# Squares of the query and key tiles: from GpSimd to ScalarE, straight from PSUM

## The reference

```
qkv = rmsnorm(x, norm_mix[0]) @ w_qkv                     # 512 x 3072
q, k -> 8 heads x 2 maps x 64 channels
q = partial_rope(rmsnorm(q, q_gain), cos, sin)            # rms over 64 channels
k = partial_rope(rmsnorm(k, k_gain), cos, sin)
a = softmax(q0 k0 / 8) - lam * softmax(q1 k1 / 8);  o = a @ v
```

## Time and profile before

| | |
|---|---|
| median of 3 runs | 981.86 us |
| lowest and highest | 980.97 and 982.65 us |
| the profiled execution | 980.41 us |
| its span, first to last instruction | 978.7 us |
| TensorE busy | 966.7 us (99%) |
| VectorE busy | 850.8 us (87%) |
| ScalarE busy | 464.0 us (47%) |
| GpSimd busy | 379.5 us (39%) |

### The profile page before, as it was taken

How to read it: one execution, slowest core, us unless ns; L and a number is a source line. 1 busy time by engine, 2 the same in 40 slices (tenths; PEclk the granted TensorE clock), 3 DMA queues, 4 the chain that set the end, 5 groups by cost and what they waited for, 6 DMA issues and landing times.

```text
span 978.7 us, 12963 instructions
## 1 busy us (share of the span) xinstructions
PE 966.7 (99%) x4684; PEld 796.8 (81%) x4684; DVE 850.8 (87%) x1157; ACT 464.0 (47%) x735; POOL 379.5 (39%) x333
## 2 busy tenths in 40 slices
PE   9999999999999999999999999999999999999998
PEld 7887888777887878888888888988888888888887
DVE  6696898999777999999989888779898988989883
ACT  6445655667456253452544534465345253452520
POOL 6941453344462828457534000551340413405000
PEclk9999999999999999999999999999999999999999
DMA  7343210200241433323333250303342333332202
GB/s 264 88 109 106 66 65 2 65 22 22 69 169 44 149 110 96 120 86 108 108 96 120 65 174 21 130 4 126 89 127 86 108 107 88 115 100 87 86 1 86
DMA packets 50967, 90.13 MB, mean 92 GB/s; under 512 B 8268, under 2 KB 9560, under 8 KB 50904
## 3 DMA queue, kind: packets, MB, share of 16 engines
q1 hardware_dynamic: 45456, 89.14, 28.6%
q10 hardware_dynamic: 5448, 0.17, 0.3%
HBM read 87.20 MB, written 2.10 MB: 91 GB/s over the span
## 4 chain that ended last, share of the span: by engine, by line
PE 63%; DVE 5%; POOL 2%; issue 1%; ACT 1%; POOLq 0%; DVEq 0%; ACTq 0%
PE bank L1718 32%; PE pair L1718 30%; POOL s_nsum L768 1%; DVE s_acc L1483 1%; DVE s_lbB_lo L1231 1%; DVE s_lt_lo L1231 1%; DVE s_w_lo L1204 1%; DVE s_acc L1552 0%; DVE s_s_raw L1468 0%; PE bank L2077 0%; DVE s_u_raw L1450 0%; PE pair L2065 0%; DVE s_hT_lo L1432 0%; POOL s_lt L794 0%; ACT s_hT_hi L1043 0%
## 5 line engine op out<-in xcount | busy, mean ns | idle before, releaser
L794 POOL TENSOR_TENSOR s_lt<-s_lbB,s_lbB 128x1024 f32<-128x1024 f32 x14 | 34.5, 2466 | 262.3 <-PE pair L1718 164.0
L1204 DVE TENSOR_TENSOR s_w_lo<-s_raw,s_w_hi 128x1024 fp32r<-128x1024 f32 x72 | 125.4, 1762 | 3.5 <-ACT s_w_hi L873 3.5
L1231 DVE TENSOR_TENSOR s_lbB_lo<-s_lbB,s_b_hi 128x1024 fp32r<-128x1024 f32 x64 | 121.3, 1920 | 0.0
L895 ACT ACTIVATE s_b_hi<-s_lbB 128x1024 fp32r<-128x1024 f32 x64 | 67.2, 1054 | 77.0 <-POOL s_lbB L794 34.1
L1718 PE MATMUL bank<-s_hT_hi,s_w_hi 128*128 128x512 f32 x256 | 100.3, 392 | 0.0
L1718 PE MATMUL pair<-s_hT_hi,s_w_hi 128*128 128x512 f32 x256 | 100.2, 391 | 0.0
L1718 PE MATMUL bank<-s_hT_hi,s_w_lo 128*128 128x512 f32 x256 | 99.7, 390 | 0.0
L1718 PE MATMUL bank<-s_hT_lo,s_w_hi 128*128 128x512 f32 x256 | 99.7, 389 | 0.0
L1718 PE MATMUL pair<-s_hT_hi,s_w_lo 128*128 128x512 f32 x256 | 99.7, 389 | 0.0
L1718 PE MATMUL pair<-s_hT_lo,s_w_hi 128*128 128x512 f32 x256 | 99.7, 389 | 0.0
L1063 ACT ACTIVATE s_u_raw<-s_u_raw 128x512 f32<-128x512 f32 x64 | 40.4, 632 | 112.1 <-DVE s_u_raw L1450 112.1
(11 more groups left out here) (269 smaller groups left out, 2708.4 us busy)
## 6 DMA issues: line engine op xcount, KB each, us to landing
s_raw<-in_mlp_w SPq DMA_DIRECT2D x64, 512.0 KB, 3.7
s_lbB<-in_mlp_w SPq DMA_DIRECT2D x64, 512.0 KB, 3.3
s_raw<-in_attn_w_qkv SPq DMA_DIRECT2D x24, 512.0 KB, 4.2
s_raw<-in_attn_w_o SPq DMA_DIRECT2D x8, 512.0 KB, 3.2
s_x_nat<-in_x SPq DMA_DIRECT2D x4, 512.0 KB, 6.2
out<-s_acc SPq DMA_DIRECT2D x7, 256.0 KB, 2.0
s_raw<-in_pool_w SPq DMA_DIRECT2D x4, 256.0 KB, 2.8
out<-s_acc SPq DMA_DIRECT2D x2, 128.0 KB, 1.8
```

The source lines that it names most:

```text
L794: g.tensor_tensor(w2_raw[n][:], w2_raw[one][:], w2_raw[two][:], ALU.subtract).then_inc(t_done, 1)
L895: a.activation(b_hi[home][:], w2_raw[n][:], ACT.Copy).then_inc(w2_hi_done, 1)
L1204: v.tensor_tensor(w_lo[slot][:, cols], raw[k][:], f32(w_hi[slot][:, cols]), ALU.subtract)\
L1231: v.tensor_tensor(w2_lo[n][:], w2_raw[n][:], f32(b_hi[home][:]), ALU.subtract).then_inc(w2_lo_done, 1)
```

## The change

ScalarE makes the squares itself: right behind the copy it reads the same PSUM bank again with the function Square and the same scale. GpSimd's `qk_square` goes. `qsq` gets a third buffer, and ScalarE waits on `qk_v_done` before it overwrites one (for tile n, until the sums of tile n - 3 are made). The semaphore `qk_copied` goes, and TensorE's waits that used it use `qk_squared`, which now counts ScalarE's squares.

```
-            def qk_square(n):
-                pool.wait_ge(qk_copied, n + 1)
-                if n >= 2:
-                    pool.wait_ge(qk_v_done, n - 1)
-                g.tensor_tensor(qsq[n % 2][:], qs[n % 4][:], qs[n % 4][:], ALU.mult).then_inc(qk_squared, 1)
...
-            qk_square(0)
-            for n in range(1, 2 * NT):
-                qk_square(n)
-                qk_root(n - 1)
-            qk_root(2 * NT - 1)
+            for n in range(2 * NT):
+                qk_root(n)
...
-                for f in range(F_V):
-                    if TAKE[f] == i:
-                        qk_square(2 * NT + f)
...
-                a.activation(qs[n % 4][:], src[:], ACT.Copy, scale=in_r[:, n % NT:n % NT + 1]).then_inc(qk_copied, 1)
+                a.activation(qs[n % 4][:], src[:], ACT.Copy, scale=in_r[:, n % NT:n % NT + 1])
+                if n >= 3:
+                    act.wait_ge(qk_v_done, n - 2)
+                a.activation(qsq[n % 3][:], src[:], ACT.Square, scale=in_r[:, n % NT:n % NT + 1])\
+                    .then_inc(qk_squared, 1)
...
-                link(v.tensor_reduce(qk_ss[:, n % 2, :], qsq[n % 2][:]. ...
+                link(v.tensor_reduce(qk_ss[:, n % 2, :], qsq[n % 3][:]. ...
...
                 if tile >= 4:
-                    pe.wait_ge(qk_copied, tile - 3)
+                    pe.wait_ge(qk_squared, tile - 3)
...
                     if 0 <= g < F_V:
-                        pe.wait_ge(qk_copied, 2 * NT + g + 1)
+                        pe.wait_ge(qk_squared, 2 * NT + g + 1)
```

More of the change, by code:

```diff
@@ L304, in build_trunk @@
             ("in_rows", [P, P], F32), ("pos_rows", [P, P], F32), ("posi", [P, P], I32))
-        qs0, qs1, qs2, qs3, qsq0, qsq1, rt0, rt1 = inside(
-            x_region, *[(f"qs{k}", [P, S], F32) for k in range(4)], ("qsq0", [P, S], F32), ("qsq1", [P, S], F32),
+        qs0, qs1, qs2, qs3, qsq0, qsq1, qsq2, rt0, rt1 = inside(
+            x_region, *[(f"qs{k}", [P, S], F32) for k in range(4)], *[(f"qsq{k}", [P, S], F32) for k in range(3)],
             ("rt0", [P, 2 * NT, ROPE], F32), ("rt1", [P, 2 * NT, ROPE], F32))
-        qs, qsq, rt = [qs0, qs1, qs2, qs3], [qsq0, qsq1], [rt0, rt1]
+        qs, qsq, rt = [qs0, qs1, qs2, qs3], [qsq0, qsq1, qsq2], [rt0, rt1]
         (val1,) = inside(x_region, ("val1", [P, 2, NT, BANK], F32R))
@@ L378, in build_trunk @@
         proj_done = sem("proj_done")
-        qk_copied = sem("qk_copied")
         qk_squared = sem("qk_squared")
@@ L1276, in qk_sum @@
                     dve.wait_ge(qk_r_done, n - 1)
-                link(v.tensor_reduce(qk_ss[:, n % 2, :], qsq[n % 2][:].rearrange("p (g d) -> p g d", d=QK), AX.X, ALU.add))
+                link(v.tensor_reduce(qk_ss[:, n % 2, :], qsq[n % 3][:].rearrange("p (g d) -> p g d", d=QK), AX.X, ALU.add))
                 v.tensor_scalar(qk_v[:, n % 2, :], qk_ss[:, n % 2, :], 1.0 / QK, EPS, ALU.mult, ALU.add)\
```

## The result

| | before | after |
|---|---|---|
| median of all runs on one chip | 981.61 us (9 runs, 980.97 to 982.65) | 984.98 us (9 runs, 982.39 to 986.67) |
| ratio after / before | | 1.0033, 95% interval 1.0022 to 1.0044 |
| profiled execution, its span | 980.41, 978.7 us | 984.98, 983.1 us |

The changed kernel is slower, by more than a measurement can hide, and the median lies above the predicted range. The nine runs fall in groups by their mean granted clock: at 1.000 982.39 and 982.95; at 0.998 four from 984.38 to 985.17; at 0.996 986.20, 986.37 and 986.67. All runs of the kernel before show 1.000.

The account below looks back on a forecast made before the run. TensorE was taken as the bound, busy 966.7 of 978.7 us with no idle in the edited stretches. Every term cost 0, so the median stayed at 981.8 us, range 980.4 to 983.3.

Parts of the forecast that it names:

- Past 165 us: After the edited stretches: VectorE's idle at 155.63 us erases any lead or lag; later timing unchanged, 5.59 us idle stays.
- What comes: 16 Squares on ScalarE, each 0.69 us long and 0.57 us of queue: 4.6 us in each of two stretches.
- the rival with its own table: Attention fillers: Square needs its own function table, so extra loads on ScalarE cost about 3 us, 984.9 us; chance 0.06.
- What goes: 16 GpSimd squares, 16.7 us, and VectorE's 7.2 us wait before its first sum; off TensorE's path, cost 0.
- TensorE's wait, projection: Projection, tile 4 needing Square 0: the square ends at 29.71 us, 2.6 us before it is needed; cost 0.
- ScalarE's new wait: Square n waiting for tile n - 3's sums: already over when reached from tile 4 on; nothing stands still.
- TensorE's wait, attention: Fillers waiting for squares: tightest is filler 7 behind filler 5's square, 0.81 us to spare; cost 0.
- ScalarE's queue, attention: Work behind filler squares: turned map 0.13 us late after 0.44 us idle, scores 1.8 us to spare; cost 0.
- VectorE freed: Rotations without GpSimd's contending squares: VectorE's lead could win TensorE 2.8 us after 191 us, 979.1 us; chance 0.04.
- Small delays: Attention: ScalarE shifts of 0.1 to 0.6 us pile up and cost TensorE up to 1 us, 982.8 us; chance 0.06.

Follow-up runs that it names:

- e5: The kernel before with 16 one-column copies added on ScalarE, squares left on GpSimd: 983.13 us, 1.0006 against the kernel before.
- e7: The changed kernel with 8 more one-column copies on ScalarE, one per filler: 983.50 us, 1.0006 against the kernel before.
- e12: The changed kernel with one more one-column copy on ScalarE and one memset on GpSimd: 980.95 us, 0.9994 against the kernel before.
- e13: The kernel before with 98 one-column memsets added on GpSimd: 983.17 us, 1.0005 against the kernel before.
- e6: The changed kernel with 30 one-column memsets on GpSimd ahead of the attention steps: 983.02 us, 1.0005 against the kernel before.
- e4: The changed kernel with six warming matmul groups (filling transposes) at the start in place of two: 982.85 us, 1.0014 against the kernel before.
- e2: The changed kernel with the dropped semaphore qk_copied kept and counted by the copy: 984.19 us, 1.0025 against the kernel before.
- e9: The changed kernel run again with no edit: 983.65 us, 1.0016 against the kernel before.
- e1: The kernel before run again with no edit: 982.27 us, 0.9999 against the kernel before.
- e3: The kernel before with only the third buffer for squares added, GpSimd still making the squares: 982.04 us, 0.9998 against the kernel before.
- e8: The changed kernel with 8 more one-column copies on ScalarE and 30 memsets on GpSimd: 982.59 us, 1.0000 against the kernel before.
- e10: The kernel before with six filling transposes at the start in place of two: 981.32 us, 0.9996 against the kernel before.
- e16: The changed kernel with one more instruction on ScalarE, one on GpSimd, and six filling transposes at the start: 981.62 us, 0.9992 against the kernel before.

## Why the prediction was wrong

It forecast 981.8 us and "same" by 0.89; the median came out at 984.98 us, slower, and the range ended at 983.3.

**The step that failed** is "Past 165 us": "From then on both programs issue the same work in the same order at the same times." Same work and order hold; the times don't. The 5.59 us of idle up to 345 us did stay (5.63 in the same stretch of the execution after), but from 165 us to the end TensorE idled 0.77 us more: 0.49 at 348.18 and 0.28 at 638.08. The runs show in its place that the start of an instruction depends on its number in its engine's queue: directly behind a released semaphore instruction, one number in 128 starts 0.28 us late. Moving 16 instructions from one queue to the other put ScalarE's 831 on a copy that TensorE waits for, 480 us behind the last square, and that delay went straight into wait B (e5 brings it, e7 and e12 take it away). It put GpSimd's 196 on a weight difference 170 us behind the last square. There the late start was hidden, and what TensorE waited for was a load that lands 0.7 to 1.2 us later beside it (e13 brings it, e6 and e12 take it away). The behaviour was in the trace of before too (GpSimd 324 at 444.25 us, ScalarE 447 at 239.78), at instructions where it cost nothing. That the delay is the switch to the next block of instructions is an inference from the transfers and the spacing; no run takes the transfer away. The Trainium skill, page "Runtime: NRT & Kernel Launch", section "Instruction fetch mechanics", says that an engine's instruction memory is refilled in 16 KiB blocks of 256 instructions and that crossing one is mostly hidden. The trace has transfers of 16 KiB too (37 of 16384 bytes on queue 8). But for ScalarE and GpSimd the traces show 8192 bytes and a recurrence at 128, and the late start isn't hidden on ScalarE's copy at wait B.

**The clock** had no term in the sum. The earlier trace rows show it at its upper level throughout, and I didn't ask what it would take to fall. In three kept traces (after, e4, e5) wait B of 0.73 us is followed, 0.4 to 2.3 us later, by 3.4 or 6.8 us at the lower level, about half of that lost. Of the other runs I have the mean clock alone: 0.998, and 0.996 or 0.997, fit one and two such lengths. By kernel:

| ScalarE's number, wait B | kernels | runs under clock 1 |
|---|---|---|
| 831, 0.73 us | after, e2, e4, e5, e6, e9 | 19 of 60 (7/9, 2/6, 4/12, 3/11, 1/11, 2/11) |
| another, 0.45 us | e1, e3, e7, e8, e10 to e16 | 0 of 109 |

The runs of the kernel before are all at 1.000 as well. e7 and e13 have wait A at 1.6 to 1.7 us and wait B at 0.45, and never fall in 19 runs, so it is wait B that matters. Four of the 18 kept traces (e3, e9, e10, e12) hold no record of the clock, so some of the runs counted as 1.000 may only lack it; in these four the matmuls' spacing behind 636 us shows no fall.

**Sizes of the loss.** 0.8 to 0.9 us in each of the four kept traces with both waits (after, e2, e4, e9), and on top the clock: in 7 of 9 runs on the first occasion, in 2 of 11 on the second. The medians' 3.4 and 1.8 us fit that roughly, with the start's spread of some 2 us on either.

**Point by point, what held.** "What comes": 0.69 us forecast, 0.683 and 0.694 measured, three table loads still; the rival with its own table is out. "What goes": no GpSimd square, and VectorE's 7.2 us of idle at the sums are 1.1. "TensorE's wait, projection" and "ScalarE's new wait": cost 0, no wait of TensorE on a square anywhere. "TensorE's wait, attention": filler 7 starts at 138.98 for 136.90, that is 2.08 later, all of it the start's; the square it waits for ran from 136.62 to 137.32, so 1.66 us were to spare where I had 0.81: the copy ahead of it had come 0.86 us earlier against TensorE, which I had taken as fixed. "ScalarE's queue, attention": the turned map behind it still stands idle, 0.73 us for 0.44. The rival "VectorE freed" had its mechanism right, and it brought nothing: VectorE's busy time fell by 6.1 us, the last step of a rotation takes 0.22 us in all 16 cases (up to 1.04 before), and at the scores of step 11 it now waits 1.78 us for TensorE where it had waited 0.86:
```profile
157.70 1.29 DVE L1345 TENSOR_REDUCE s_nmax<-pair 128x1 f32<-128x512 f32 x2 [1.78 <-PE pair L1709]
...
193.31 0.49 PE L1709 MATMUL pair<-s_qkT_hi 64*128 64x512 f32 x2 [0.70 <-ACT s_p L991]
```
The lead ends there, and the wait of the earlier trace rows is 0.70 us to the digit. "Small delays" looked in the wrong place: not piled up in attention, but by single instructions far behind.

**The range** took the spread of three runs of before, 1.7 us. The 129 runs of the kernel before in the four later comparisons spread over 2.3 to 3.2 us in each. In the kept traces most of that is the start: the clock is up at 8.43 us in the execution before and at 13.27 in e1, the same kernel, which is 2.6 us of their 2.9.

**Open.** Why a wait of 0.73 us is followed by a lower clock in some executions and not in others, and why in 7 of 9 runs once and 2 of 11 later. Whether GpSimd's transfer of instructions slows the load behind wait A, or both follow from something else. And in 13 of the 17 other traces, of either kernel, TensorE falls back another 0.15 to 0.3 us between 346 and 500 us against the execution before: by execution, it seems, and unexplained.

## What to carry to other kernels

Adding or removing instructions moves everything behind them in that engine's queue: where a few awaited instructions bound the time, compare traces partner by partner and look at which number they have, and try one dummy instruction before blaming the edit. Follow the late row to what really holds the next one: at wait A the late start was hidden, and a load behind it was not. On a kernel whose engine is full, a change of a few tenths per cent may come from a stage that wasn't edited; judge the edit only after such placement is evened out. And ask of a full TensorE not only what would stop it but also whether a pause that grows is followed by a fall of its clock.

## What the runs showed of the hardware that I had not expected

In ScalarE's and GpSimd's queue one instruction in 128, if it stands directly behind a semaphore instruction at which its engine had idled, starts 0.28 us late (0.34 for 0.06 us in 26 of 26 cases, 0.42 for 0.14 in 14 of 15), and an 8192-byte transfer of instructions follows its start, mostly by 0.65 to 0.96 us. A 512 KB load under way when GpSimd has such an instruction took 4.05 to 4.28 us for 3.07 to 3.33. An idle of TensorE of 0.73 us near 636 us went with a granted clock of 0.50 soon after it (3.4 or 6.8 us long in three traces) in 19 of 60 executions; 0.45 us in the same place in none of 109. Idles of 1.0 to 1.7 us near 346 us preceded none in the kept traces.
